# One encoder layer step on one core: a small gate product behind the first dot products, the v rows spread anew over the u rows, and the last dense pass mixed with two tiles' token products

## What is computed

```
q = h2 @ w_query ; s1, s2 = q-halves . sub_keys          # 8 heads, 128 keys in each half
best 16 of the 16x16 sums of the best 16 + 16  -> idx, gate = softmax
act = gelu(h2 . u_tab[idx])                              # 16 rows of u per head and token
y   = sum over heads and k of gate * act * v_tab[idx]    # 16 rows of v per head and token
x   = x + gate2 * RMSNorm(y) * g_post2
```

## Time and profile before

| | us |
|---|---|
| median of three runs | 3760.28 |
| lowest, highest | 3757.12, 3773.67 |
| the profiled execution, its own time | 3764.5 |
| its span, first to last instruction | 3762.7 |
| PE, DVE, POOL, ACT busy in it | 3049.4, 2338.3, 1659.7, 910.5 |

### The profile page before, as it was taken

How to read it: one execution, slowest core, us unless ns; L and a number is a source line. 1 busy time by engine, 2 the same in 40 slices (tenths; PEclk the granted TensorE clock), 3 DMA queues, 4 the chain that set the end, 5 groups by cost and what they waited for, 6 DMA issues and landing times.

```text
span 3762.7 us, 30958 instructions
## 1 busy us (share of the span) xinstructions
PE 3049.4 (81%) x8866; PEld 1320.3 (35%) x8866; DVE 2338.3 (62%) x6337; ACT 910.5 (24%) x2020; POOL 1659.7 (44%) x1710
## 2 busy tenths in 40 slices
PE   8999899993987855566546999956774899998998
PEld 2454455561432210022134444423223444442222
DVE  3102555394897788899899778777769876520000
ACT  1001677221221111145254100024325210000000
POOL 0000400022456667767634444457763444416665
PEclk9999899996999988988856999979995899999999
DMA  9300510323799999999988999999997999969998
GB/s 351 109 24 25 152 22 0 126 80 140 258 330 392 387 398 408 403 399 400 404 266 280 408 405 405 404 334 408 407 401 268 346 406 409 406 234 349 376 393 328
DMA packets 347355, 1132.66 MB, mean 301 GB/s; under 512 B 49478, under 2 KB 71238, under 8 KB 345002
## 3 DMA queue, kind: packets, MB, share of 16 engines
q0 software_dynamic: 239776, 872.55, 60.7%
q1 hardware_dynamic: 91280, 228.93, 16.5%
q10 hardware_dynamic: 16128, 29.22, 2.2%
HBM read 1099.77 MB, written 30.79 MB: 300 GB/s over the span
## 4 chain that ended last, share of the span: by engine, by line
PE 35%; DMA 17%; DVE 10%; POOL 6%; issue 5%; ACT 3%; ACTq 0%; SPq 0%; DVEq 0%; POOLq 0%
PE ps_y L1985 20%; DMA urow<-in_u_tab,idx 12%; PE ps_y L2000 9%; DVE urow L1885 5%; POOL urow L1571 3%; DMA vrow<-in_v_tab,idxT 3%; POOL vrow L1582 3%; PE ps_g L2013 3%; PE ps_y L1931 2%; ACT keys_sb L1719 1%; DVE keys_sb L1869 1%; ACT keys_sb L1721 1%; ACT G L1737 1%; DMA G<-h_d 1%; DMA s_d<-G 0%
## 5 line engine op out<-in xcount | busy, mean ns | idle before, releaser
L1885 DVE CUSTOM_DVE_ANT_0 urow<-urow,ps_h 128x1024 f32<-128x1024 f32 x1088 | 1323.4, 1217 | 399.7 <-DMA urow<-in_u_tab,idx 382.7
L1571 POOL DMA_INDIRECT urow<-in_u_tab,idx x1024 | 965.7, 943 | 848.3 <-DVE dots L1885 721.7
L2000 PE MATMUL ps_y<-vrow,keys_sb 128*32 128x512 f32 x2048 | 782.8, 651 | 223.4 <-DMA vrow<-in_v_tab,idxT 214.2
L1985 PE MATMUL ps_y<-vrow,G 128*128 128x512 f32 x2048 | 885.1, 595 | 1.4 <-ACT G L1737 1.4
L1582 POOL DMA_INDIRECT vrow<-in_v_tab,idxT x576 | 542.4, 942 | 321.7 <-PE ps_y L2000 165.7
L1985 PEld LDWEIGHTS ps_y<-vrow,G 128*128 128x128 f32 x2048 | 390.9, 191 | 491.9 <-issue 490.0
L2013 PE MATMUL ps_g<-keys_sb 128*128 128x128 f32 x1024 | 213.4, 374 | 295.6 <-DVE keys_sb L1869 158.7
L2000 PEld LDWEIGHTS ps_y<-vrow,keys_sb 128*32 128x32 f32 x2048 | 178.2, 115 | 761.2 <-issue 457.6
L2013 PEld LDWEIGHTS ps_g<-keys_sb 128*128 128x128 f32 x1024 | 182.7, 268 | 386.4 <-DVE keys_sb L1869 274.3
L1850 DVE TENSOR_SCALAR msq<-msq 128x1 f32<-128x1 f32 (+1 forms) x9 | 1.3, 148 | 419.6 <-ACT rs L1752 419.6
L1931 PE MATMUL ps_y<-G 128*128 128x512 f32 x512 | 230.3, 606 | 0.7 <-ACT G L1786 0.7
(11 more groups left out here) (220 smaller groups left out, 3102.1 us busy)
## 6 DMA issues: line engine op xcount, KB each, us to landing
vrow<-in_v_tab SPq DMA_DIRECT2D x256, 512.0 KB, 6.7
ada<-in_w_ada SPq DMA_DIRECT2D x12, 2048.0 KB, 13.1
urow<-in_u_tab,idx POOLq DMA_INDIRECT x1024, 7.8
vrow<-in_v_tab,idxT POOLq DMA_INDIRECT x576, 6.7
w_in_sb<-in_w_in SPq DMA_DIRECT2D x8, 1024.0 KB, 18.1
G<-in_w_query SPq DMA_DIRECT2D x8, 1024.0 KB, 15.1
s_d<-G SPq DMA_DIRECT2D x16, 512.0 KB, 9.7
sc<-s_d ACTq DMA_DIRECT2D x64, 128.0 KB
```

The costliest lines, as they stand in the source:

```text
L1571: nc.gpsimd.indirect_dma_start(urow[s % RU][:, :], None, A["u_tab"][:, :], bass.IndirectOffsetOnAxis(ap=places[:, col:col + 1], axis=0)).t ...
L1885: nc.vector.tensor_tensor_reduce(out=urow[s % RU][:, :], in0=urow[s % RU][:, :], in1=ps_h[:, :], scale=1.0, scalar=0.0, op0=ALU.mult, op1= ...
L1985: last = nc.tensor.matmul(ps_y[x][:, f], G[x][:, b, :], vrow[v % RV][:, f], start=(b == 0), stop=(b == NKEY - 1))
L2000: last = nc.tensor.matmul(sums(n)[r, f], W[:, b, 31 - a:63 - a], vrow[v % RV][:, f], start=(a == 0), stop=(a == 31), skip_group_check=True)
```

## The change

1. SP's two small loads for the gate product go ahead of the eight loads of h2, and DVE does the product at the second unit, behind the first eight dots. The transpose of tile 0's indices moves from slot 2 to slot 30.
2. `DUE`: tile 1's products are spread over slots 200 to 504 (before: 200 to 456); pair 0's blocks begin at 528 (526); tile 4's products are spread over 732 to 890 (746 to 852); behind slot 1006 items fall due at 1.15 a slot (0.64), so that 606 are due by the last dot (564). `BURST` of tile 5 begins at 738 (748). `NORM`, `FINISH`, `STORE`, `H2_AFTER` follow.
3. The last 64 blocks of pair 1 are mixed with the products of tiles 7 and 8: three products, one block, 64 times; then the last 64 products.
4. Tile 7 is summed in `ps_g`, tile 8 in `ps_h` (before both in `ps_y`), so they no longer wait for tiles 5 and 6 to be finished; tile 7 waits for the last group and for tile 8's index transpose, tile 8 for its weights, which are transposed in `ps_h`. The norms of tiles 5, 6 and 7 come behind the last block.

```diff
-    tokens(0)
-    tokens(1)
-    blocks(0)
-    tokens(4)
-    blocks(1)
-    tokens(7)
-    tokens(8)
-    DUE = [(0, 0), (72, 0), (192, 64), (200, 64), (456, 192), (526, 192), (716, 320), (746, 320), (852, 448), (908, 448),
-           (NU, 564)]
+    ITEMS = tokens(0) + tokens(1) + blocks(0) + tokens(4)
+    behind, last_blocks = tokens(7) + tokens(8), blocks(1)
+    ITEMS += last_blocks[:64]
+    for b in range(64):
+        ITEMS += behind[3 * b:3 * (b + 1)] + last_blocks[64 + b:65 + b]
+    ITEMS += behind[192:]
...
+    DUE = [(0, 0), (72, 0), (192, 64), (200, 64), (504, 192), (528, 192), (716, 320), (732, 320), (890, 448), (908, 448),
+           (1006, 512), (NU, 606)]
...
-    BURST = {2: (330, 3), 3: (459, 2), 5: (748, 2), 6: (838, 2)}
+    BURST = {2: (330, 3), 3: (459, 2), 5: (738, 2), 6: (838, 2)}
...
-    NORM = {205: 0, 470: 1, 728: 2, 738: 3, 864: 4}
-    FINISH = {213: 0, 478: 1, 732: 2, 742: 3, 870: 4}
+    NORM = {205: 0, 512: 1, 722: 2, 732: 3, 896: 4}
+    FINISH = {213: 0, 518: 1, 726: 2, 737: 3, 902: 4}
...
-            T_SLOT[first(n) + 40 if n else 2] = (n, "idx")
+            T_SLOT[first(n) + 40 if n else 30] = (n, "idx")
...
         def sums(n):
-            return ps_y[{0: 0, 1: 1, 2: 0, 3: 1, 4: 0, 5: 0, 6: 1, 7: 0, 8: 1}[n]]
-        BEFORE = {2: 0, 3: 1, 4: 2, 5: 4, 6: 3, 7: 5, 8: 6}
+            return {0: ps_y[0], 1: ps_y[1], 2: ps_y[0], 3: ps_y[1], 4: ps_y[0], 5: ps_y[0], 6: ps_y[1], 7: ps_g, 8: ps_h}[n]
+        BEFORE = {2: 0, 3: 1, 4: 2, 5: 4, 6: 3}
...
+            sp.dma_start(gains[0:2, :], A["rows"][2:3, :].broadcast_to([2, D])).then_inc(gain_in, 16)
+            sp.dma_start(io[0:2, :], S["mod_d"][0:2, 5 * D:6 * D]).then_inc(gain_in, 16)
             for t in range(NT):
...
-                if g >= RW:
-                    act.wait_ge(v_used, v - (RW - 1) * quads)
-                elif n > 1:
-                    act.wait_ge(v_used, begin[n])
+                if g >= RW or n > 1:
+                    act.wait_ge(v_used, through[m - RW])
...
-                if v == end[5] + 5:
+                if v == end[5] + 8:
                     norm(5)
+                elif v == end[5] + 12:
                     store(5)
-                elif v == end[5] + 9:
                     norm(6)
+                elif v == end[5] + 20:
                     store(6)
-                elif v == end[7] + 5:
                     norm(7)
+                elif v == end[5] + 28:
                     store(7)
...
-            dve.wait_ge(gain_in, 32)
-            nc.vector.tensor_tensor(io[0:2, :], io[0:2, :], gains[0:2, :], ALU.mult).then_inc(gain_done, 1)
...
+                if q == 1:
+                    dve.wait_ge(gain_in, 32)
+                    nc.vector.tensor_tensor(io[0:2, :], io[0:2, :], gains[0:2, :], ALU.mult).then_inc(gain_done, 1)
...
-                    if a == b == 0 and n >= 2:
+                    if a == b == 0 and n == 1:
+                        pe.wait_ge(q_copied, 4 * PH)
+                    elif a == b == 0 and n == 4:
                         pe.wait_ge(y_done, BEFORE[n] + 1)
-                    elif a == b == 0 and n == 1:
-                        pe.wait_ge(q_copied, 4 * PH)
+                    elif a == b == 0 and n == 7:
+                        pe.wait_ge(g_evac, groups(dense[-1], NGRP))
+                        pe.wait_ge(t_copied, t_event(8, "idx") + 1)
+                    elif a == b == 0 and n == 8:
+                        pe.wait_ge(t_copied, t_event(8, "w") + 1)
```

More of the change, by code:

```diff
@@ L1382, in experts @@
     unit = {u: q for q, u in enumerate(UNITS)}
-    ITEMS, begin, end = [], {}, {}
     def tokens(n):
[L1388 to L1391, removed]
+        return [(n, g, a) for g in range(32) for a in range(4 if n else 2)]
     def blocks(p):
-        for n in PAIRS[p]:
-            begin[n], end[n] = len(ITEMS), len(ITEMS) + NKEY
-        ITEMS.extend((None, p, c) for c in range(NKEY))
-    tokens(0)
-    tokens(1)
-    blocks(0)
-    tokens(4)
-    blocks(1)
-    tokens(7)
-    tokens(8)
-    DUE = [(0, 0), (72, 0), (192, 64), (200, 64), (456, 192), (526, 192), (716, 320), (746, 320), (852, 448), (908, 448),
-           (NU, 564)]
+        return [(None, p, c) for c in range(NKEY)]
+    ITEMS = tokens(0) + tokens(1) + blocks(0) + tokens(4)
[4 more added lines that the diff above has]
+    ITEMS += behind[192:]
+    begin, end = {}, {}
+    for v, (n, a, b) in enumerate(ITEMS):
+        for x in (PAIRS[a] if n is None else (n,)):
+            begin.setdefault(x, v)
+            end[x] = v + 1
+    DUE = [(0, 0), (72, 0), (192, 64), (200, 64), (504, 192), (528, 192), (716, 320), (732, 320), (890, 448), (908, 448),
+           (1006, 512), (NU, 606)]
     def due(s):
@@ L1431, in groups @@
         return dense.index(n) * NGRP + g
-    NORM = {205: 0, 470: 1, 728: 2, 738: 3, 864: 4}
-    FINISH = {213: 0, 478: 1, 732: 2, 742: 3, 870: 4}
-    STORE = {217: 0, 482: 1, 734: 2, 746: 3, 874: 4}
+    NORM = {205: 0, 512: 1, 722: 2, 732: 3, 896: 4}
+    FINISH = {213: 0, 518: 1, 726: 2, 737: 3, 902: 4}
+    STORE = {217: 0, 522: 1, 728: 2, 741: 3, 906: 4}
     GATE = {2: 0, 4: 1, 6: 2, 7: 4, 8: 5}
-    H2_AFTER = {220: 3, 485: 5, 750: 7, 877: 8}
+    H2_AFTER = {220: 3, 525: 5, 745: 7, 909: 8}
     def t_event(n, what):
@@ L1533, in wgroup @@
         def wgroup(v):
-            return sum(32 for n in (0, 1, 4, 7, 8) if end[n] <= v) + ITEMS[v][1]
+            return 32 * (0, 1, 4, 7, 8).index(ITEMS[v][0]) + ITEMS[v][1]
+        through = {wgroup(v): v + 1 for v, (n, _, _) in enumerate(ITEMS) if n is not None}
         def target(q):
@@ L1548, in _ @@
                 sp.dma_start(h2ld[t % 2], S["h2_d"][t * P:(t + 1) * P, :]).then_inc(h2ld_in[t % 2], 16)
-            sp.dma_start(gains[0:2, :], A["rows"][2:3, :].broadcast_to([2, D])).then_inc(gain_in, 16)
-            sp.dma_start(io[0:2, :], S["mod_d"][0:2, 5 * D:6 * D]).then_inc(gain_in, 16)
             sp.wait_ge(gain_done, 1)
@@ L1669, in take_w @@
                 at = HALF + P
+                ps_t = ps_h if n == NT else ps_g
                 if n in dense:
@@ L1679, in take_w @@
                     w = P if n else DEC
-                    nc.scalar.activation(wT[n % 2][:, 0:w], ps_g[:, at:at + w], ACT.Copy).then_inc(t_copied, 1)
+                    nc.scalar.activation(wT[n % 2][:, 0:w], ps_t[:, at:at + w], ACT.Copy).then_inc(t_copied, 1)
             def put_w(v):
@@ L1963, in turn @@
                         srcs = [ij[n % 2][:, 0, :], ij[n % 2][:, 1, :]] + srcs
+                ps_t = ps_h if (n, what) == (NT, "w") else ps_g
                 for i, src in enumerate(srcs):
                     if n:
-                        last = nc.tensor.transpose(ps_g[:, c + P * i:c + P * (i + 1)], src, ident)
+                        last = nc.tensor.transpose(ps_t[:, c + P * i:c + P * (i + 1)], src, ident)
                     else:
@@ L1969, in turn @@
                             r = slice(DEC * half, DEC * (half + 1))
-                            last = nc.tensor.matmul(ps_g[r, c:c + DEC], src[r, 0:DEC], ident[r, r], start=True,
+                            last = nc.tensor.matmul(ps_t[r, c:c + DEC], src[r, 0:DEC], ident[r, r], start=True,
                                                     stop=True, skip_group_check=True)
```

## The result

The changed kernel takes **3724.88 us** (median of four executions, 3721.2 to 3729.03) against 3762.07 for the kernel before beside it (four, 3757.12 to 3773.67): a ratio of 0.9897, 95% interval 0.988 to 0.9915. That is 37 us less; the prediction said 3713 and 47.5 less. The profiled execution took 3729.03, its span 3727.2.

A forecast was written before the change was run, and what follows sets the result against it. DMA at about 403 GB/s (1.30 us an item) bounds most stretches, DVE the bursts, PE also the last stretches. Terms -3 + 18 - 2.5 + 31 + 4 = 47.5 us won, from 3760.3 to 3713 us; range 3655 to 3764.

The forecast's parts named there:

- the dips of the middle: Bursts of tiles 3 and 6, DMA at 247 and 263 GB/s without v items; moved products should lift it over 350.
- the ring holds the rounds: Behind the last dot, six v buffers hold one and a half rounds of three products and a block: 6.7 us each.
- start, to slot 200: Moved gate product: gain 0, early gathers delay h2 loads and PE's queries; 0 to 8 us lost, 3 taken.
- tile 1's spread, burst of tile 3, blocks two slots later (200 to 528): 0.42 products a slot for 0.5 wins 18 us; 19 products in tile 3's burst cost 0; later blocks lose 2.5.
- 528 to 738, and 738 to 907: Slot 738 comes 1.5 us later than 743 had; slots 738 to 907 take 410 us for 442.8: 31 won.
- from slot 908: Nothing changes to slot 1006; then 229 us to the last dot and 373 behind it, 602 for 606: 4 won.
- The rival of the bursts: Bursts of tiles 3, 5 and 6: products hold up groups at 1.2 GHz; 80 us more, 3793; chance 0.08.
- the forecast's own sign of being wrong: At the start, PE's queries beginning over 8 us later would show the forecast wrong.
- R: Time of one round (three products, a block) behind the last dot: (2.0 + landing time + 5.35)/2, taken as 6.7 us.
- its first rival: Behind the last dot, gathers land in 3.3 us, rounds go at 5.35: 55 us less, 3658; chance 0.17.
- about 0.1 us: PE's cost per change between full-width and strip products, read from the first strip product beside a group's end; not summed.
- an estimate of 3.2 us: Landing of a 512 KB gather from POOL by the skill: 2.0 us plus its bytes at 436 GB/s; trace 6.0.

The follow-up runs named there:

- the plain pass: Changed kernel with last pass unmixed (all blocks, then products): 3712.8 us with six buffers; with eight buffers and gate product back at the start, 3682.79 us.

## Why the prediction was right, and where its sum was off

The sign holds, and so do the two main readings: the dips of the middle are filled, and the ring holds the rounds. The sum missed by 12 us. That it missed by no more is partly luck: the last part came out 19 us worse than forecast, and the middle 8 better. By its own steps (measured from slot to slot between the two profiled executions, and from the spans at the end):

| step of the sum | predicted | measured |
|---|---|---|
| start, to slot 200 | 3 lost | 4.3 lost (6.8 at slot 64), 1.8 of it ahead of the first h2 load; 3.9 and 4.2 by the two runs that undo it |
| tile 1's spread, burst of tile 3, blocks two slots later (200 to 528) | 18 - 2.5 = 15.5 won | 22.0 won |
| 528 to 738, and 738 to 907 | 31 won | 32.6 won |
| from slot 908 | 4 won | 14.8 lost |
| sum | 47.5 won | 35.5 won |

**The middle** was sized well, and the run with the old spread shows that it carries the whole gain: 48.4 us by its trace. Slots 216 to 329 won 12.1 for 12, slots 738 to 907 took 408.6 for 410, and slot 738 came 1.6 us later behind slot 528 than slot 743 had before, for 1.5. Tile 1's spread gave more than 18 mainly in slots 426 to 458, 7.4 for 3.5, where the new rate let go of DMA's 404 GB/s altogether (392). The burst of tile 3 carried its 19 products for nothing, as taken, and a little less.

**The rival of the bursts** (products hold up the groups at half clock, 3793) is out. In the two bursts, while products and groups run together, the changed kernel reads (all engines: length, PE, PEld, DVE, ACT and POOL busy, clock, DMA share, GB/s; the last three rows are slots 1006 to 1087, the rounds, and the last 64 products):

```profile
1867.40:1966.50 99.10, 67.98 (x253) 31.78 (x253) 97.77 (x299) 60.09 (x146) 61.20 (x65) 0.90 0.98 365
2731.70:2857.00 125.30, 89.94 (x379) 39.11 (x377) 113.09 (x339) 72.11 (x178) 87.40 (x92) 0.92 1.02 402
...
3105.50:3331.00 225.50, 207.44 (x478) 59.88 (x477) 101.21 (x170) 3.75 (x23) 140.48 (x151) 1.00 1.02 408
3335.00:3610.00 275.00, 269.99 (x789) 85.59 (x784) 0.00 (x0) 6.32 (x30) 110.38 (x118) 1.00 0.86 299
3621.10:3716.20 95.10, 88.17 (x257) 22.76 (x256) 9.60 (x18) 11.31 (x28) 55.22 (x59) 0.98 0.96 364
```

The granted clock is 0.90 and 0.92 there, where the whole bursts had 0.50 and 0.54, the lower level (1.2 GHz, 0.50) nearly throughout. A slot takes 99.1/45 = 2.20 us and 125.3/52 = 2.41, so the groups come every 4.4 and 4.8 us, as the forecast's 4.86 had it and not 5.9. With the old spread the clock is at 0.51 and 0.54 again.

**The start** lost what was taken, for the reason given: the loads land later, the scores with them. It was near the forecast's own sign of being wrong, queries over 8 us later: they start at 940.80, and in the kernel before at

```profile
932.93 5.54 PE L1931 MATMUL ps_y<-G 128*128 128x512 f32 x8 [0.69 <-ACT G L1786]
```

That is 7.9 us later, of which 1.8 were there before SP's first h2 load.

**The step that failed is the sum from slot 908**, 15 lost for 4 won: the mix, forecast as a small gain, was a loss with six buffers. Slots 1006 to 1087 were right (225.5 us for 229). The rounds were mis-sized: R was put at 6.7 and measured 7.01, and there were 42 of them where 40.5 had been counted; from the last dot to the first of the last 64 products it took 3621.1 - 3331.0 = 290 us for 2 + 271 = 273, 17 more. The last 64 products took 95.1 us, 1.49 each and not 1.40: 5.6 more. What I had left out of R is only partly known. With the measured numbers in the same formula (products 2.0, landing 5.7 at the median, and PE's own 5.49 for 5.35) it gives (2.0 + 5.7 + 5.49) / 2 = 6.6, so 0.4 stays open. POOL issues gathers in one order and stood 94.0 us behind blocks, so a free buffer may wait behind one that is not free; that was not tried by itself. That the ring holds the rounds at all, on which the forecast and its first rival differed, is shown: two buffers more bring 45 us, to 3680, a good part of the way to that rival's 3658.

A turn of PE cost 0.34 us for its two changes of matmul shape; "about 0.1 us" from rows 8 was too low, and the sum had no term for it. The Trainium skill (TensorEngine Tiling (Array Packing), Key Properties) says that such a change drains TensorE. The traces agree that there is a stop, of 0.17 us here. Over 42 rounds that is 14 us where PE paces them, less where the ring does.

In the trough at 299 GB/s (DMA share 0.86), a quarter below the 408 beside the dots (share 1.02), the gathers landed in 5.7 us at the median and never under 4.1. The Trainium skill (DMA: Bandwidth & Descriptors, Anatomy of one DMA), from which the prediction worked out an estimate of 3.2 us, is not borne out by these rows either.

## What to carry to other kernels

Where two kinds of work with different limits are mixed, count how many buffers one turn of the mix needs while its longest item holds one: here the mix lost 12 us with six buffers and was no longer a loss with eight, and two more buffers were worth 45 us in it. Time that a trace shows as a dip in a shared resource (DMA at 247 GB/s between stretches at 403) can be won by moving work in from the neighbours, and the gain can be priced from those rows alone: 43.5 us forecast by slot 908, 50.3 found. An item started sooner wins nothing when the next wait is for something else, and its traffic may delay just that.

## What had not been expected

- PE's clock rose where work was *added*: the bursts went from 0.50 and 0.54 to 0.90 and 0.92 with products between the groups, while slots 216 to 329, with fewer products, went from 0.90 to 0.81. What the clock alone was worth was not tried: in the first burst DVE was busy 97.77 of 99.10 us, and at the lower clock 146.36 of 153.00.
- A product that comes late loses more than its wait: 1.88 us alone, where three that start together take 2.08 in all.
- With eight buffers DMA carries 407 GB/s for gathers alone behind the last dot, as much as beside the dots (408); the 374 of the earlier trace rows, which I took for the pace of landings, was below that; in the plain pass two more buffers raised it from 377 to 407.
